# A hybrid attention layer on one core: softmax units, query turns and root computations moved to other slots

## The reference

```python
h = rmsnorm(x, ln_gain)
proj = h @ w_in                      # 2048 x 5376, split in:
# q_a 1024, k_a 128, v_a 128, g_a 1024 | b, c, xh, g_c 512 each | q_m, g_m 512 each
o_a = swa_sink_attention(q_a, k_a, v_a, ...)   # 16 heads of 64, chunks of 64, 128 keys, sinks, bias
o_c = b * causal_dwconv3(c * xh)
o_m = memory_cross_attention(q_m, mem_h, ...)  # 4 heads of 128, 256 memory tokens
mixed = concat(silu(g_a) * o_a, silu(g_c) * o_c, silu(g_m) * o_m)
out = x + mixed @ w_out
```

## Time and profile before

| | |
|---|---|
| median of 3 runs | 2729.85 us (2726.09 to 2733.01) |
| profiled execution, its own time | 2726.99 us |
| its span | 2725.1 us |
| PE busy | 98% of the span |
| DVE, ACT, POOL busy | 62%, 40%, 55% |
| mean granted clock of PE | 0.996 |

### The profile page before, as it was taken

The page is one execution under the profiler, slowest core; times in us unless marked ns, Lnnn a source line. Parts: engine busy times, 40 slices in busy tenths (PEclk is TensorE's granted clock), DMA queues, the critical chain, the costliest instruction groups (busy, mean ns, idle before and its releaser), DMA issues.

```text
span 2725.1 us, 33717 instructions
## 1 busy us (share of the span) xinstructions
PE 2666.0 (98%) x12475; PEld 2198.8 (81%) x12475; DVE 1686.9 (62%) x2504; ACT 1101.5 (40%) x2435; POOL 1496.5 (55%) x1042
## 2 busy tenths in 40 slices
PE   6999999999999999999999999999999999999999
PEld 4888877888887778888877888888788788888887
DVE  4345775664476666456675754457642787867667
ACT  6333434442344344333434442343343444444443
POOL 5555644546554445555544455555454775756766
PEclk9999999999999999999999999999999999999999
DMA  7344443534344344334433434344245454444534
GB/s 216 122 138 124 159 135 97 174 110 161 106 138 151 112 143 142 129 119 140 159 120 113 155 124 139 113 132 151 92 150 168 157 199 146 167 150 140 174 118 140
DMA packets 234408, 383.16 MB, mean 141 GB/s; under 512 B 16822, under 2 KB 76292, under 8 KB 231940
## 3 DMA queue, kind: packets, MB, share of 16 engines
q1 hardware_dynamic: 189748, 274.05, 32.3%
q10 hardware_dynamic: 44496, 106.96, 11.1%
HBM read 308.86 MB, written 46.92 MB: 131 GB/s over the span
## 4 chain that ended last, share of the span: by engine, by line
PE 75%; DVE 13%; issue 3%; ACT 3%; DMA 2%; SPq 2%; POOL 1%; ACTq 0%; DVEq 0%
PE acc L1491 18%; PE acc L1493 17%; PE acc L1492 17%; DVE early L1146 4%; PE acc L1558 3%; PE acc L1562 3%; PE acc L1560 3%; ACT probs L779 1%; DMA probs_t<-blocks_t 1%; SPq L443 1%; PE ps_s L1615 1%; PE ps_o L1641 1%; DVE blocks_t L1221 1%; DMA raw<-in_w_mem_kv 1%; DVE a_lo L1362 1%
## 5 line engine op out<-in xcount | busy, mean ns | idle before, releaser
L536 POOL TENSOR_TENSOR w_lo<-raw,w_hi 128x512 fp32r<-128x512 f32 x928 | 1311.3, 1424 | 1168.6 <-ACT w_hi L620 1166.2
L620 ACT ACTIVATE w_hi<-raw 128x512 fp32r<-128x512 f32 x928 | 571.0, 628 | 1112.8 <-PE acc L1493 795.9
L1491 PE MATMUL acc<-h_hi,w_hi 128*128 128x512 f32 x1792 | 707.3, 395 | 12.8 <-POOL w_lo L536 10.7
L1492 PE MATMUL acc<-h_lo,w_hi 128*128 128x512 f32 x1792 | 700.4, 391 | 0.0
L1493 PE MATMUL acc<-h_hi,w_lo 128*128 128x512 f32 x1792 | 700.2, 391 | 0.0
L1491 PEld LDWEIGHTS acc<-h_hi,w_hi 128*128 128x128 f32 x1792 | 337.8, 188 | 91.6 <-POOL w_lo L536 13.8
L1493 PEld LDWEIGHTS acc<-h_hi,w_lo 128*128 128x128 f32 x1792 | 337.9, 189 | 70.9
L1492 PEld LDWEIGHTS acc<-h_lo,w_hi 128*128 128x128 f32 x1792 | 337.8, 189 | 68.7
L1491 PE MATMUL acc<-w_hi,h_hi 128*128 128x512 f32 (+1 forms) x1024 | 379.7, 371 | 0.0
L1493 PE MATMUL acc<-w_hi,h_lo 128*128 128x512 f32 (+1 forms) x1024 | 372.1, 363 | 0.0
L1492 PE MATMUL acc<-w_lo,h_hi 128*128 128x512 f32 (+1 forms) x1024 | 371.4, 363 | 0.0
(11 more groups left out here) (232 smaller groups left out, 3575.3 us busy)
## 6 DMA issues: line engine op xcount, KB each, us to landing
raw<-in_w_in SPq DMA_DIRECT2D x336, 512.0 KB, 4.0
raw<-w_sums SPq DMA_DIRECT2D x64, 512.0 KB, 3.9
probs_t<-blocks_t SPq DMA_DIRECT2D x384, 64.0 KB, 2.1
raw<-in_w_out SPq DMA_DIRECT2D x48, 512.0 KB, 3.6
stage<-in_w_out ACTq DMA_DIRECT2D x16, 1024.0 KB, 5.3
w_sums<-stage ACTq DMA_DIRECT2D x16, 1024.0 KB, 4.2
stage<-in_x ACTq DMA_DIRECT2D x16, 1024.0 KB, 5.1
mixed_rows<-ungated ACTq DMA_DIRECT2D x12, 1024.0 KB, 4.3
```

Source lines behind the costliest of these rows:

```text
L536: nc.gpsimd.tensor_tensor(w_lo[:, at, :], raw[:, slot_mod, HALF * half:HALF * half + HALF], w_hi[:, at, :].bitcast(F32), ALU.subtract).the ...
L620: nc.scalar.activation(w_hi[:, 2 * (slot_mod % 2) + half, :], raw[:, slot_mod, HALF * half:HALF * half + HALF], ACT.Copy).then_inc(hi_read ...
L1491: nc.tensor.matmul(dst, st[0], mv[0], start=first, stop=False)
L1492: nc.tensor.matmul(dst, st[0], mv[1], start=False, stop=False)
```

## The change

Six things move, and nothing is added to the computation.

- The eight memory units' scores go from slots 16 to 23 to slots 17 to 24, with all their later steps. The last local unit's scores (u = 23) go from slot 64 to 65; its values come in slot 68, for which PE's loop over the gates now also calls `values`, and its move in slot 71.
- The transposition of the second local queries (kind 2) is in four parts of 8 instructions in slots 40, 41, 42 and 45, not two of 16 in 45 and 46.
- The convolution blocks go from slots 47 to 50 to slots 46 to 49.
- The root of x on POOL has its own table: for n = 1, 2 and 3 it is in POOL's slot 46, 72 and 75, where it was in 45, 71 and 74; the mean stays. The scaling for n = 1 goes from slot 46 to 53; the load and squares of n = 2 from 68 and 70 to 69 and 71.
- The fourth weight sum goes from load 39, sum 45, store 46 to 47, 54, 55.
- In the output stage ACT's wait and load stand at the start of slot 2 of each 28, not of slot 0.

```diff
--- before.py
+++ after.py
@@ -74,18 +74,20 @@
 RSQRT_AT = {FLOW0: (0, 0), FLOW0 + 11: (1, 0), FLOW0 + 12: (1, 1),
             FLOW0 + 22: (2, 0), FLOW0 + 23: (2, 1)}
 SCALE_AT = {FLOW0 + 1: 0, FLOW0 + 12: 1, FLOW0 + 25: 2}
-Q_TURN_AT = {FLOW0 + 1: (0, 0), FLOW0 + 2: (0, 1), FLOW0 + 13: (1, 0), FLOW0 + 14: (1, 1),
-             FLOW0 + 33: (2, 0), FLOW0 + 34: (2, 1)}
+Q_TURN_AT = {FLOW0 + 1: (0, 0, (0, 4)), FLOW0 + 2: (0, 1, (0, 4)),
+             FLOW0 + 13: (1, 0, (0, 4)), FLOW0 + 14: (1, 1, (0, 4)),
+             FLOW0 + 28: (2, 0, (0, 2)), FLOW0 + 29: (2, 0, (2, 4)),
+             FLOW0 + 30: (2, 1, (0, 2)), FLOW0 + 33: (2, 1, (2, 4))}
 K_TURN_SLOT = 6
 
 
-SCORES_AT = {FLOW0 + 4 + u: u for u in range(8)}
+SCORES_AT = {FLOW0 + 5 + u: u for u in range(8)}
 SCORES_AT.update({FLOW0 + 17 + 2 * u: 8 + u for u in range(8)})
-SCORES_AT.update({FLOW0 + min(39 + 2 * u, 52): 16 + u for u in range(8)})
+SCORES_AT.update({FLOW0 + 39 + 2 * u: 16 + u for u in range(8)})
 MOVE_AT = {s + 6: u for s, u in SCORES_AT.items()}
 SPLIT_AT = {s + 2: u for s, u in SCORES_AT.items() if u >= 8}
 VALUES_AT = {s + 3: u for s, u in SCORES_AT.items()}
-CONV_AT = {FLOW0 + 35 + b: b for b in range(4)}
+CONV_AT = {FLOW0 + 34 + b: b for b in range(4)}
 
 LAST_SLOT = {}
 _s = 0
@@ -122,10 +124,11 @@
 
 
 X_TILES = (3, 0, 2, 1)
-X_LOAD_AT = {24: 0, 38: 1, 68: 2, 72: 3}
-X_SQUARE_AT = {27: 0, 44: 1, 70: 2, 74: 3}
+X_LOAD_AT = {24: 0, 38: 1, 69: 2, 72: 3}
+X_SQUARE_AT = {27: 0, 44: 1, 71: 2, 74: 3}
 X_MEAN_AT = {28: 0, 45: 1, 71: 2, 74: 3}
-X_SCALE_AT = {29: 0, 46: 1, 72: 2, 75: 3}
+X_RSQRT_AT = {28: 0, 46: 1, 72: 2, 75: 3}
+X_SCALE_AT = {29: 0, 53: 1, 72: 2, 75: 3}
 X_FLIP_AT = {29: (0, 0, 6), 31: (0, 6, 10), 35: (0, 10, 13), 37: (0, 13, 16),
              70: (1, 0, 6), 71: (1, 6, 13), 72: (1, 13, 16),
              73: (2, 0, 7), 74: (2, 7, 16),
@@ -134,9 +137,9 @@
 H_SPLIT_END = (14, 15)
 
 
-T_LOAD_AT = {7: 0, 12: 1, 31: 2, 39: 3}
-T_SUM_AT = {9: 0, 28: 1, 36: 2, 45: 3}
-T_STORE_AT = {10: 0, 29: 1, 37: 2, 46: 3}
+T_LOAD_AT = {7: 0, 12: 1, 31: 2, 47: 3}
+T_SUM_AT = {9: 0, 28: 1, 36: 2, 54: 3}
+T_STORE_AT = {10: 0, 29: 1, 37: 2, 55: 3}
 
 
 MIX_STORE_AT = {63: 0, 71: 1, 79: 2}
@@ -576,8 +579,8 @@
                         cols = slice(16 * part, 16 * part + 16)
                         rsqrt(q_scale[:, cols], q_mean[:, cols], 16, q_meaned, g * 3 + kind + 1,
                               q_rstd)
-                    if s in X_MEAN_AT and g < GROUPS - 1:
-                        x_item(2 + TT + g * TT + X_MEAN_AT[s])
+                    if s in X_RSQRT_AT and g < GROUPS - 1:
+                        x_item(2 + TT + g * TT + X_RSQRT_AT[s])
 
             def add_resid(r, to, t, made, loaded):
 
@@ -912,7 +915,7 @@
 
             for j in range(OUT_SLOTS):
                 r, at = j // PAIR_SLOTS, j % PAIR_SLOTS
-                if at == 0:
+                if at == 2:
                     act.wait_ge(mixed, GROUPS * 16 + 1)
                     if r:
                         act.wait_ge(resid_added, 12 * r)
@@ -1127,13 +1130,13 @@
                 nc.vector.tensor_tensor(q, q, q_scale[:, 0:n].unsqueeze(2).broadcast_to(
                     [P, n, 2048 // n]), ALU.mult).then_inc(q_normed, 1)
 
-            def turn_queries(g, kind, part):
-
-                if part == 0:
+            def turn_queries(g, kind, part, rows_in):
+
+                if part == 0 and rows_in[0] == 0:
                     dve.wait_ge(q_normed, g * 3 + kind + 1)
 
                 rows = ungated[:, q_blocks(kind), :].rearrange("p t (b c) -> p t b c", c=P)
-                for i in range(4):
+                for i in range(*rows_in):
                     for j in range(4):
                         if kind == 0:
                             cols = early[:, q_blocks(0), :].rearrange("p b (t q) -> p t b q", q=P)
@@ -1146,7 +1149,8 @@
                         last = nc.vector.transpose(
                             to, rows[32 * i:32 * i + 32, :, 2 * part:2 * part + 2,
                                      32 * j:32 * j + 32])
-                last.then_inc(q_turned, 1)
+                if rows_in[1] == 4:
+                    last.then_inc(q_turned, 1)
 
             def probs_low(g, u):
                 dve.wait_ge(pt_high, g * 16 + u - 7)
@@ -1708,8 +1712,10 @@
                         at += 1
                 for n in range(LAST_GATES):
                     for s in range(SB_SLOTS):
-                        feature_slot(s, s % 2, base + GATE_SLOT0 + n * SB_SLOTS + s,
-                                     g * USES + n + MEM_USES + len(BLOCKS))
+                        at = GATE_SLOT0 + n * SB_SLOTS + s
+                        feature_slot(s, at % 2, base + at, g * USES + n + MEM_USES + len(BLOCKS))
+                        if at in VALUES_AT:
+                            values(g, VALUES_AT[at])
             for j in range(OUT_SLOTS):
                 product_slot(j)
```

## The result

The changed kernel takes 2762.03 us (median of 4 executions, 2761.45 to 2764.42). The kernel before took 2731.43 us beside it (4 executions, 2726.09 to 2736.40). The ratio is 1.012, 95% interval 1.0106 to 1.0134: slower by 1.1 to 1.3%. The forecast was 2752, or +0.8%: direction and mechanism as forecast, the difference 8.5 us too small (22.1 us forecast, 30.6 measured).

The account below looks back on a forecast made before the run. PE is 98% busy, so only its waits and clock move time. 23.2 + 19.8 + 5.4 + 9.6 - 36.3 = +21.7 us on 2726.99 gives 2748.7; adding 2.9 for the median, 2752, range 2742 to 2764.

Parts of the forecast that it names:

- product X, slot 44: Slot 44, four groups: query transposes ahead of the product of X with C on DVE make PE late, 23.2 us.
- gate, slot 76: Slot 76, three groups: the n = 3 root behind w_lo on POOL delays DVE's scaling and gate, 19.8 us.
- what was taken away: Five existing causes of PE waits, fourteen waits in all, removed together with four slow-clock stretches: 36.3 us saved.
- Clock: Behind seven new PE waits over 4 us: 1.6 us of slow clock charged to six, 9.6 us.
- the rule cited there: Trainium skill: every long enough idle gap returns PE to half rate; all seven new waits would pay, 11.2 us.
- Unit 23 in slot 68: Slot 68, four groups: pt_lo behind DVE's gate ends 1.36 us after the slot's matmuls could use it, 5.4 us.
- n = 2 in slot 72 blocks DVE likewise, but no bank waits there: Slot 72: scaling of x for n = 2 holds DVE as for n = 3, but PE loses nothing.
- Product X in time: Rival at slot 44: DVE has room for the transposes, no wait and no clock loss there; 2723 us, 7 in 100.
- the gate in time: Rival at slot 76: POOL's root comes early enough or scaling does not block; 2728 us, 8 in 100.
- neither: Rival: no new wait at slot 44 or 76, only the removed waits count; 2699 us, 5 in 100.
- The fourth: Rival: a further w_lo wait in slots 36 to 42, 6 us in four groups; 2776 us, 8 in 100.

Follow-up runs that it names:

- run 1: Changed kernel with the second local queries transposed in two parts of 16 in slots 45 and 46 again: 2734.5 us, ratio 1.002.
- run 2: Changed kernel with the root of x for n = 3 back in POOL's slot 74, ahead of w_lo: 2743.28 us, ratio 1.0059.
- run 10: Changed kernel with only unit 23's values moved, to slot 69 instead of 68: 2750.45 us, ratio 1.0075.
- run 4: Changed kernel with second local queries, root of n = 3 and unit 23's scores and values all back at their old places: 2706.28 us, ratio 0.9922.
- run 5: Run 4 with load, squares and root of x for n = 2 also back at their old slots: 2700.26 us, ratio 0.9889.
- run 8: Kernel before with only the root of x for n = 1 in slot 46 and its scaling in slot 53: 2726.21 us, ratio 0.9986.
- run 6: Run 5 with unit 23's scores in slot 65 and its values in slot 69: 2691.97 us, ratio 0.9860.
- run 9: Changed kernel with run 5's and run 6's edits for x and unit 23's values, query parts in slots 40, 44, 45, 46: 2691.73 us, ratio 0.9861.
- run 7: Kernel before with only the eight memory units' scores a slot later, in slots 17 to 24: 2724.83 us, ratio 0.9982.

## Why the prediction came out as it did

Direction and places were right: each of the three new waits is where the prediction put it, for the reason it gave, and runs 1, 2 and 10 each take one away by one edit (run 2 all but 1.9 us of it). The forecast sum was +21.7; the spans lie 37.4 apart. Term by term, in idle time with 0.16 us for each wait:

| term | forecast | measured | how |
|---|---|---|---|
| product X, slot 44 | 23.2 | 26.3 | 25.7 + 4 x 0.16 |
| gate, slot 76 | 19.8 | 18.8 | 18.8 + 3 x 0.16, less the 0.16 us it was late before, three times |
| pt_lo, slot 68 | 5.4 | 9.7 | 10.4 less unit 19's 1.3, and 4 x 0.16 |
| clock behind the new waits | 9.6 | 19.3 | the eight windows above |
| what was taken away | -36.3 | -35.8 | the output keeps 0.6 + 0.16; stretches at 1.2 GHz had cost 6.6, not 6.4 |
| sum | 21.7 | 38.3 | spans: 37.4 |

The 0.9 us by which the sum goes over the spans were not traced.

**The step that failed most is "Clock": its term was 9.6 us and measured 19.3.** It charged one stretch of 1.6 us to six of seven waits. All seven have a loss behind them, of 2.0 to 3.2 us each (0.71 to 0.55 in the windows), 17.6 us together, and one of the four waits at slot 68 has another 1.6. The 1.6 us came from waits of 4.4 us and less; behind 4.8 to 7.0 us more was lost each time in this profile. So both the number of stretches and their price were too low, and the upper bound given, 22.4 us, was nearer than the value taken. By the rule cited there every long wait pays. The 31 waits of 4.4 us and over behind 100 us, in all profiles of this case, all have such a loss behind them. The rule was the better guide for these, and the doubt raised from two waits of 3.1 us did not bear on them. It would not have mended the price: at 1.6 us each, seven stretches are 11.2 us. This profiled execution had the lowest mean granted clock of its four, 0.988 against 0.989 and 0.990; for the others the term is by an estimate from these clocks (0.001 to 0.002 of the span) 3 to 5 us smaller, still well over 9.6.

**"Unit 23 in slot 68" was mis-sized.** pt_lo begins 6.06 us after the slot does (1028.39, against 1030.19 - 2.26 - 0.16 - 5.44), within 0.1 us of the forecast, but lasts 1.75 us and not 0.69. The price had been taken from an instance with nothing beside it on POOL. The Trainium skill (GPSIMD Engine Reference, section 1. Specifications) has GpSimd share its SBUF interfaces with VectorE and collide with DVE instructions that have two inputs in SBUF, as pt_lo has; the trace agrees, with 1.06 us more on pt_lo and 0.75 on the two w_lo. No run moved w_lo away from pt_lo on purpose, but among the 423 pt_lo with no w_lo beside them none took over 0.70 us.

**Product X** was 3 us more, within the bound given: PE could begin 7.1 us late in group 1 (6.98 + 0.16), where 6.3 were forecast. DVE came 0.5 us later against PE than before: the transposition of the probabilities began 2.93 us ahead of the time slot 44 was due (870.83), and 3.47 ahead of it before. That PE no longer waits in slot 16, to which the prediction gave a bound and then nothing, is the likely reason; it was not tried alone. The other 0.3 us are small terms: the second part began 1.14 us behind that transposition, where `attention_sum` had begun 1.02 behind it; the gaps between the blocks; and 0.84 us from the product's start to the matmul, not 0.7. **The gate** was 1 us less.

**One sentence was wrong and cost nothing in the sum:** "n = 2 in slot 72 blocks DVE likewise, but no bank waits there". No bank does there, but three slots on the mean of n = 3 is late behind the 16 transposes, and the gate behind that. Runs 2 and 4 show it at 1.9 us in three groups, and run 5 removes it. It was hidden behind the larger wait at the same place, so it did not count here and would have counted in a forecast of the repair: of the 11 us by which run 4 was short, run 5 won 6.0 back.

**What was taken away** came out at its price, though the reason given for slot 48 was incomplete. The prediction named DVE's 8 transposes and POOL's root. Run 1 shows that having fewer transposes in slot 45 is not needed for it, and run 8 that the root alone frees slot 48 and makes slot 52 wait instead. Product B's wait is gone in run 1 too, with all 16 transposes back, but DVE is not ahead of PE there (0.04 us between the convolution and product B), and runs 5 and 6 have one such wait each. With the four parts of run 9 DVE is 1.4 to 4.0 us ahead. What convolution and weight sum do for it separately is not settled.

**The range.** 2742 to 2764 contains the measured time, but its upper end adds only the clock's bound; with the 7.6 us that the prediction itself allowed for product X it would have been 2772.

**The rivals.** "Product X in time" falls with the 25.7 us, "the gate in time" with the 18.8, "neither" with both. The fourth, new w_lo waits in slots 36 to 42, has no such wait. 2699 was named for "neither new wait"; with the same moves placed well (run 9) it is 2691.7, so the moves could have brought what they suggest, with unit 23's values a slot later and the load, squares and roots of n = 2 and 3 as they were.

## What to carry to other kernels

Before an instruction is moved into an engine's list, read what stands behind it there and who waits for that: two blocks of transposes, 7.2 us together, cost PE 7.0 us of idle time in front of product X and nothing three slots on, and a root of 0.55 us cost 6.3 us behind a w_lo. Where PE is 98% busy, the clock is a term of its own: each wait beyond 4 us cost 1.5 to 3.1 us more. And a removed wait counts fully only when the next one in line is looked at too (runs 4, 7 and 8): compute the second-latest arrival at each place, for it is what stays. Last, the same instructions of one engine can take longer when another engine's work is moved beside them: pt_lo 1.75 us for 0.69, a convolution 15.4 for 14.2.

## What the hardware showed that was not expected

**How likely a wait of PE is to bring a stretch at 1.2 GHz grows with its length.** Over the thirteen profiles, the waits of PE behind 100 us fall into these classes by idle time, with those that have a stretch below full clock behind them (read from the granted clock), and what one cost:

| idle, us | waits | with a loss | cost of one, us |
|---|---|---|---|
| 0.8 to 1.2 | 22 | 0 | |
| 1.2 to 1.85 | 18 | 4 | 1.7 |
| 1.85 to 2.2 | 8 | 3 | |
| 2.3 (pt_lo) | 12 | 5 | 1.6 to 1.7 |
| 2.8 to 3.3 | 12 | 9 | 1.5 to 3.0, mean 2.0 |
| 3.4 to 3.6 | 3 | 3 | 1.6 to 3.1, mean 2.1 |
| 4.4 to 5.3 | 7 | 7 | 1.5 to 3.1, mean 2.3 |
| 6.3 | 12 | 12 | 1.8 to 3.1, mean 2.5 |
| 7.0 | 12 | 12 | 1.6 to 3.0, mean 2.2 |

Most classes are one or two places in the kernel (all of 6.3 us are at slot 76, all of 7.0 at slot 44), so length and place are not told apart by this table. Place or its surroundings do matter: in the class of 1.2 to 1.85 us, the twelve waits for the memory queries, 1.8 us each, had no loss behind them, and four of the other six had. What decides between a loss and none behind a wait of 1.3 to 3.3 us was not found.

It is also much of the scatter. The two kernels with no wait over 0.5 us in the groups (runs 6 and 9) lie within 1.0 us from lowest to highest. The kernel before, with its fourteen waits, spreads over 10 us, and its time goes with its clock: in the executions timed beside the experiments, 2725.7 to 2726.4 us at a mean granted clock of 0.998, and 2733.0 to 2736.0 at 0.992 and below.
